# Transformer block with expert retrieval on one core: the last sublayer and the query run once per 128-token tile, the second tile on plain float32 weights

## The chip, the cores and the metric

The kernel runs on one core of one Trainium2 chip. The metric is the device time of one execution in microseconds (us), the median of several runs. It is written by hand: each engine has its own program, and the engines meet only at semaphores. TensorE (PE) does the matrix products, VectorE (DVE) and ScalarE (ACT) the elementwise work, GpSimd (POOL) and SyncE (SP) issue transfers.

## The reference, cut to what matters

256 tokens of width 2048 pass through two layers of a first block (layers 0 and 1 below), then a mixer sublayer and a retrieval sublayer of a second block. 16 meta tokens stand ahead of the tokens in the second block. The change touches only the second block:

```
h = x;  16 meta tokens ahead of it
proj = rms_norm(h) @ w_in            # 2048 x 7176: sb_q sb_k sb_v fq fk fv fgate flogit
sb   = stick_breaking_attention(...)  # 8 heads of 128, causal
fox  = forgetting_attention(...)      # 8 heads of 128, causal, q and k normed per head
h    = h + concat(rms_norm(sb), rms_norm(fox) * sigmoid(fgate)) @ w_out      # 2048 x 2048
hb   = rms_norm(h)
q    = hb @ w_query                   # 2048 x 2048 -> 8 heads, 2 halves of 128
s    = q . sub_keys;  top 16 of each half, top 16 of the 256 sums -> idx (8 heads x 16), g = softmax
a    = gelu(u[idx] . hb);  out = h + sum (g * a) * v[idx]                    # u, v: 16384 x 2048
```

Attention is causal, so the first 128 tokens need nothing of the last 128.

## The kernel before, in words

**Passes.** Seven products of all 256 tokens with a weight matrix follow each other, numbered p = 0 to 6: `w_in` and `w_out` of layer 0 and 1 (p 0 to 3), then `w_in_2` (4), `w_out_2` (5) and the query weights (6). `GROUPS` cuts the columns of each into groups of up to 512; `PIECES` cuts each group into 8 pieces of 256 rows. A piece is one load of 512 KB (256 rows x 512 columns) into one of the 4 slots of `ring` (SP queue). `split` on ACT copies it to `wH` (float32r, a rounded float), `split` on DVE writes the rest, raw minus `wH`, to `wL`; there are three buffers of each (`NB`). `piece` on PE then makes each product as three float32r products (`three`: high by high, high by low, low by high) for the two token tiles t = 0 and 1, into banks `pp`. The left factor, `hH` and `hL`, is made ahead by `chunk` (PE transposes, ACT rounds, DVE subtracts), four rows of 128 at a time. SP's wait is for a free ring slot: a slot is free when DVE has split it, and in the key and value groups of p 4 only when PE has also read it for the meta tokens (`piece_meta`, plain float32 on the raw weights).

**Order.** One generator, `order`, is walked by all five engine programs. Between the pieces `pump` steps the lanes X, Y and M, generators that do the attention a little at a time: `stick` and `fox_pair` in p 4, both tiles together. All engines are in order, so an engine that waits in a lane step holds up its next piece.

**Retrieval.** `scores` and `choose` find the experts for a group of 32 picks per token (i = 0 to 7; i // 4 is the tile). `dot` is a gather of 128 rows of `u` (1 MiB, an indirect transfer that POOL issues) and one DVE multiply-and-sum of 128x2048; `vmix` is four such gathers of `v` and 16 PE products. Each gather takes one of `NG` = 11 slots `gs`. There are 256 gathers of u and 256 of v. The first 20 dots stand beside the last pieces of p 6, all else after them. `hidden` makes the normed tokens `hn` that a dot needs, `blend` the weights of a vmix.

Of the kernel before, what the change touches and what calls it, by code (L numbers as in the profile page):

```python
# [27 lines left out]
GBP, FHP = (QI, 6144)  # L28
NP = 6488
SQ, SK, SV, FQ, FK, FV, FG, FL = (0, 1024, 2048, 3072, 4096, 5120, 6144, 7168)  # L30
MSK, MSV, MFK, MFV, MFL = (0, 1024, 2048, 3072, 4096)

ID, ONE, TRL, TRU, NTT, SM, NSM, INV, CUT, SEL, ROW, NCW = (0, 128, 256, 384, 512, 640, 768, 896, 976, 980, 996, 1000)
# [5 lines left out]
def constants():  # L39
# [14 lines left out]
    cw[:, SEL:SEL + 16] = (i[:, None] % 32) == 16 + np.arange(16)[None, :]  # L54
# [95 lines left out]
def cgroups(*spans):  # L150
# [23 lines left out]

def order():

    owed = {"X": 0.0, "Y": 0.0, "M": 0.0}
    where = [(p, q) for p in range(7) for q in range(len(PIECES[p]))]
# [15 lines left out]
    def project(p, after, rates, early, beside=lambda n, pc: ()):  # L194
        for q, (n, c0, w, pc) in enumerate(PIECES[p]):
# [5 lines left out]
            if p == 4 and meta_part(c0, w):  # L201
                yield "meta", p, q
# [9 lines left out]
            if p == 4 and n == 0 and pc == 1:  # L212
                yield "chunk", p, 3
            yield from pump(*rates(n))

    LATE = {1: {2: 3}, 3: {2: 3}, 5: {1: 2, 3: 3}}
# [64 lines left out]
    def after_in2(n):  # L281
        if n == 2:
            yield "open", "X", "forget"
        if n in (3, 9):
            yield "open", "Y", "stick", n // 9
        if n in (4, 10):
            yield "open", "X", "fox_turn", n // 10, FQ
        if n in (6, 12):
            yield "open", "X", "fox", n // 12
        if n == 13:  # L290
            yield "open", "X", "fox_rms"
        if n == 14:
            yield "drain", "X", "Y"
            yield "fox_gate",

    def beside_in2(n, pc):
        if n == 0 and pc == 3:
            yield "norm", 4
        if n and pc == 3:
            yield "drain", "M"  # L300
        if n in (6, 12) and pc == 3:
            yield "open", "X", "fox_turn", n // 12, FK

    def early_out2(pc):
        if pc == 1:
            yield "drain", "Y"
            yield "chunk", 5, 0
        if pc == 3:
            yield "chunk", 5, 1
# [14 lines left out]
    for q, (g, c0, w, pc) in enumerate(PIECES[6]):  # L324
        yield from splits(6, q)
        if q == 3:
            yield "norm", 6
# [2153 lines left out]
```

## Time and profile before

| | |
|---|---|
| runs | 3119.54, 3122.51, 3128.95 us (median 3122.51) |
| profiled execution, first to last instruction | 3121.8 us |
| PE, DVE, ACT, POOL busy | 67%, 59%, 27%, 26% of the span |
| moved by the transfers | 900.90 MB |
| p 4 begins on PE | 1157.5 us |
| first gather | 1797.4 us |
| last gather lands | 3110.8 us |

The span of 3121.8 us is 0.7 us under the median of the runs, so sums made on the profiled execution stand for the runs as well. "Beside" means on another engine or queue in the same stretch. A MATMUL row's duration is longer than the distance to the next one, since products overlap in the array; a stream is priced by the distance of starts. A plain float32 product shows as two rows, a float32r product as one.

### The profile page before, as it was taken

Reading aid. Unit: us, or ns where it says so; the run is one execution under the profiler, and the core shown is the slowest. Engines: PE = TensorE matmul, PEld = TensorE weight load, DVE = VectorE, ACT = ScalarE, POOL = GpSimd, SP = SyncE. Lnnn points to the kernel's source line nnn. Section 1 sums busy time; section 2 is a strip of 40 time slices with the busy share of each in tenths; the row PEclk is TensorE's granted clock in tenths of the full one; section 3 lists DMA queues with packets and bytes.
Section 4 is the critical chain, followed back from the end, with each engine's and each line's share of the span. In section 5 each row is a group of like instructions: output and inputs, shape, how many; then the busy total and the mean of one; then the engine's idle time right before and its main releaser. Section 6 shows DMA issues by size and latency. Waiting matters only on the chain.

```text
span 3121.8 us, 29077 instructions
## 1 busy us (share of the span) xinstructions
PE 2089.0 (67%) x11378; PEld 1478.6 (47%) x11378; DVE 1836.5 (59%) x2711; ACT 853.8 (27%) x1267; POOL 800.9 (26%) x680
## 2 busy tenths in 40 slices
PE   5888989989999999999999983223232322322235
PEld 2676777888787787666668871000000000000001
DVE  3679886566776664343336697766565555564430
ACT  1334544444454454544545420000000000000000
POOL 1111110000000000000000036665555555555552
PEclk8999999999999999999999996566656566666667
DMA  9887875557665545334226699999999999999998
GB/s 385 289 293 263 296 259 150 184 182 248 210 189 153 164 158 172 111 122 132 85 82 201 194 377 403 422 422 421 421 422 421 422 421 419 421 421 421 421 421 346
DMA packets 244741, 900.90 MB, mean 289 GB/s; under 512 B 20759, under 2 KB 45613, under 8 KB 178413
## 3 DMA queue, kind: packets, MB, share of 16 engines
q0 software_dynamic: 94208, 612.85, 48.9%
q1 hardware_dynamic: 149152, 284.53, 27.8%
q8 instruction: 90, 1.47, 0.2%
q10 hardware_dynamic: 1244, 1.67, 0.2%
q14 instruction: 47, 0.38, 0.0%
HBM read 894.78 MB, written 2.10 MB: 287 GB/s over the span
## 4 chain that ended last, share of the span: by engine, by line
PE 45%; DMA 29%; DVE 10%; ACT 3%; issue 3%; POOL 2%; ACTq 0%; POOLq 0%; DVEq 0%
PE pp L1818 38%; DMA late<-in_peer_v,MI 9%; DMA P<-in_peer_v,MI 5%; PE tp L1818 5%; DMA x<-in_peer_v,MI 5%; DMA ring<-in_peer_v,MI 4%; DVE wL L1130 3%; DMA SY<-in_peer_v,MI 2%; PE tp L1821 2%; ACT wH L626 1%; DMA ring<-in_peer_w_query 1%; DVE UHM L1286 1%; DMA ring<-in_w_in 1%; POOL late L2361 1%; DVE P L1777 0%
## 5 line engine op out<-in xcount | busy, mean ns | idle before, releaser
L1130 DVE TENSOR_TENSOR wL<-ring,wH 128x1024 fp32r<-128x1024 f32 (+3 forms) x504 | 583.2, 1161 | 573.7 <-ACT wH L626 572.4
L1818 PE MATMUL pp<-wH,hH 128*128 128x512 f32 (+3 forms) x1888 | 745.7, 395 | 35.5 <-DVE wL L1130 19.4
L1818 PE MATMUL pp<-wL,hH 128*128 128x512 f32 (+3 forms) x1888 | 721.4, 382 | 0.0
L1818 PE MATMUL pp<-wH,hL 128*128 128x512 f32 (+3 forms) x1888 | 720.5, 382 | 0.0
L626 ACT ACTIVATE wH<-ring 128x1024 fp32r<-128x1024 f32 (+3 forms) x504 | 508.3, 1011 | 729.7 <-PE pp L1818 548.0
L1818 PE MATMUL pp<-late,S 128*32 128x512 f32 x768 | 232.6, 879 | 335.7 <-DMA x<-in_peer_v,MI 156.3
L1818 PEld LDWEIGHTS pp<-wH,hH 128*128 128x128 f32 x1888 | 362.3, 192 | 141.2 <-issue 46.3
L1818 PEld LDWEIGHTS pp<-wH,hL 128*128 128x128 f32 x1888 | 361.6, 192 | 64.1
L1818 PEld LDWEIGHTS pp<-wL,hH 128*128 128x128 f32 x1888 | 362.8, 192 | 57.3 <-issue 1.0
L1777 DVE CUSTOM_DVE_ANT_0 late<-late,P 128x2048 f32<-128x2048 f32 x84 | 191.2, 2288 | 155.2 <-DMA late<-in_peer_u,MI 155.2
L1818 PE MATMUL pp<-P,S 128*32 128x512 f32 x360 | 162.7, 898 | 166.9 <-DMA late<-in_peer_v,MI 93.2
L1818 PEld LDWEIGHTS pp<-late,S 128*32 128x32 f32 x768 | 52.1, 154 | 441.3 <-issue 441.3
L1818 PE MATMUL pp<-ring,S 128*32 128x512 f32 x344 | 156.7, 890 | 142.3 <-DMA late<-in_peer_v,MI 142.3
L1818 PE MATMUL pp<-x,S 128*32 128x512 f32 x376 | 165.1, 880 | 126.2 <-DMA P<-in_peer_v,MI 65.8
L2371 POOL DMA_DIRECT2D P<-in_w_mod x85 | 44.9, 529 | 634.2 <-DVE hL L1173 314.3
L1818 PE MATMUL pp<-SY,S 128*32 128x512 f32 x200 | 140.3, 867 | 89.8 <-DMA P<-in_peer_v,MI 89.8
L1029 ACT ACTIVATE MI<-MI 128x32 f32<-128x32 f32 x8 | 1.8, 229 | 640.3 <-DVE MI L1697 640.3
L1777 DVE CUSTOM_DVE_ANT_0 P<-P 128x2048 f32<-128x2048 f32 x53 | 121.0, 2288 | 93.4 <-DMA P<-in_peer_u,MI 93.2
L2361 POOL DMA_INDIRECT late<-in_peer_v,MI x96 | 117.6, 1225 | 173.5 <-PE pp L1818 149.4
L1777 DVE CUSTOM_DVE_ANT_0 x<-x,P 128x2048 f32<-128x2048 f32 x49 | 111.9, 2289 | 78.9 <-DMA x<-in_peer_u,MI 78.9
L2347 POOL DMA_DIRECT2D UHM<-in_norm_ffn x1 | 0.5, 533 | 605.6 <-PE pp L1818 605.6
L1777 DVE CUSTOM_DVE_ANT_0 ring<-ring,P 128x2048 f32<-128x2048 f32 x47 | 107.2, 2288 | 75.7 <-DMA ring<-in_peer_u,MI 75.7
(305 smaller groups left out, 2985.2 us busy)
## 6 DMA issues: line engine op xcount, KB each, us to landing
ring<-in_w_in SPq DMA_DIRECT2D x288, 512.0 KB, 4.4
ring<-in_w_out SPq DMA_DIRECT2D x96, 512.0 KB, 4.2
P<-in_w_mod POOLq DMA_DIRECT2D x85, 512.0 KB, 5.1
late<-in_w_mod SPq DMA_DIRECT2D x64, 512.0 KB, 9.4
SY<-in_w_mod POOLq DMA_DIRECT2D x43, 512.0 KB, 5.5
ring<-in_w_in SPq DMA_DIRECT2D x48, 368.0 KB, 4.8
ring<-in_peer_w_query SPq DMA_DIRECT2D x32, 512.0 KB, 7.9
ring<-in_w_in SPq DMA_DIRECT2D x24, 344.0 KB, 3.2
```

The costliest lines, as they stand in the source:

```text
L626: act(heads(wH[k % NB][:, 0:2 * wd], 2), raw, ACT.Copy).then_inc(*tick("act_hi", ("hi", k)))
L1029: act(c3, c3, ACT.Exp).then_inc(*tick("act_x", ("gap exp", i)))
L1130: tt(lo, raw, hi.bitcast(F32), ALU.subtract).then_inc(*tick("dve_lo", *names))
L1286: stt(mod_acc, wv, c, mod_acc, ALU.mult, ALU.add).then_inc(*tick("dve_side", *names))
L1777: e.tensor_tensor_reduce(out=gs[slot], in0=gs[slot], in1=hn[i // 4], scale=1.0, scalar=0.0, op0=ALU.mult, op1=ALU.add, accum_out=aa[i % 2] ...
L1818: return e.matmul(o, l, r, start=start, stop=stop, skip_group_check=skip)
L1821: return e.transpose(o, i, ident[0:k, 0:k])
L2347: e.dma_start(to, src).then_inc(*landed(sem, *names))
L2361: e.indirect_dma_start(gs[slot], None, tab[0], bass.IndirectOffsetOnAxis(ap=picks, axis=0)).then_inc(*landed(f"expert_in{slot}", ("gathere ...
L2371: e.dma_start(mod_in[b], I["w_mod"][l, k * 128:(k + 1) * 128, c0:c0 + 1024]).then_inc(*landed(f"mod_in{b}", ("mod", m)))
```

## The change

Passes 4 to 6 become six passes of one tile each: 4, 5, 6 for tokens 0 to 127, then 7, 8, 9 for tokens 128 to 255, over the same three weight matrices, which are so loaded twice. Groups are 1024 columns wide (the first 344, one 688), and a piece is one row block of 128 by the group's width: 16 pieces to a group, 192 pieces a tile. Tile 0 keeps the split into `wH` and `wL`. Tile 1 has no split: its pieces multiply the raw weights in `ring` by `hB`, float32. The attention lanes do four heads (tile 0) or two (tile 1) of one tile at a time in both lanes. In passes 7 to 9, 128 dots (all u gathers of tile 0) are dealt out at 0.68 to a piece; for them there are 6 gather slots, and 13 after pass 9. Scores, choice, `hidden` and the transposed sub-keys are made per tile; the v gathers of tile 0 come after pass 9.

```diff
-G_IN2 = cgroups((FG + 688, 1, 344), *[(c + 512 * h, 1, 512) for h in range(2) for c in (SQ, SK, SV, FQ, FK, FV)],
-                (FG, 2, 344))
-GROUPS = [G_IN, G_OUT, G_IN, G_OUT, G_IN2, G_OUT, G_OUT]
-PIECES = [[(n, c0, w, pc) for n, (c0, w) in enumerate(g) for pc in range(8)] for g in GROUPS]
-NB, NS, NG = 3, 4, 11
-FIRST_DOT = 12
+G_IN2 = [(FG + 688, 344), (FQ, 1024), (FK, 1024), (FV, 1024), (FG, 688), (SQ, 1024), (SK, 1024), (SV, 1024)]
+G_OUT2 = [(0, 1024), (1024, 1024)]
+GROUPS = [G_IN, G_OUT, G_IN, G_OUT, G_IN2, G_OUT2, G_OUT2, G_IN2, G_OUT2, G_OUT2]
+BOTH = 4
+NPC = [8] * BOTH + [16] * 6
+NB, NS, NG = 3, 4, 13
+SHARE = 0.68
...
+    def dot(share):
+        dots[1] += share
+        while dots[1] >= 1:
+            dots[1] -= 1
+            if dots[0] < 32 * min(chosen[0], 4):
+                yield "dot", dots[0] // 32, dots[0] % 32
...
+    for p in (4, 7):
+        t, share = tile_of(p), 0 if p == 4 else SHARE
+        for q, (n, c0, w, pc) in enumerate(PIECES[p]):
...
+            if p == 7 and (n, pc) == (0, 8):
+                yield from choice(1)
+            yield "piece", p, q
...
+            yield from pump(*((0.8, 0.8, 1) if p == 4 else (0.7, 0.7, 1)))
+            yield from dot(share)
...
+            if n == 0 and pc == 3:
+                for k in range(14 if t else 0):
+                    yield "step", "X"
+                    yield "step", "Y"
+                    yield from dot(1)
+                yield "drain", "X", "Y"
+                yield "open", "Y", "stick_norm", t
...
+    yield "rest",
+    yield "turn_q", 9, 1
+    yield "scores", 6
+    yield "scores", 7
+    yield "open", "X", "choose", 4
+    yield "blend", 0
+    for b in range(8):
+        yield "vmix", 0, b
...
+        hB = late[:, 2048:4096].rearrange("p (k n) -> p k n", k=NK)
...
             def split(p, q):
                 n, c0, wd, pc = PIECES[p][q]
-                r, k = next(loads), next(cut)
-                raw = heads(ring[:, r % NS, 0:2 * wd], 2)
+                r = next(loads)
+                if p >= 7:
+                    return
+                k, size = next(cut), 2 * wd if p < BOTH else wd
...
+            def piece_one(p, q):
+                n, c0, wd, pc = PIECES[p][q]
+                k, r, kk = next(cut) if p < 7 else None, raw_of[p, q], row_of(p, n, pc)
+                w.wait_ge(*(at("lo", k) if p < 7 else at("raw", r)))
+                w.wait_ge(*at("chunk", p, kk // 4))
+                for j, (o, wj) in enumerate(sides(wd)):
+                    b = bank_of(p, n, j)
+                    if pc == 0 and b in had_bank:
+                        w.wait_ge(*at(*had_bank[b]))
+                    if p < 7:
+                        m = three(pp[b][:, 0:wj], (hA[0][:, kk, :], hA[1][:, kk, :]),
+                                  (wH[k % NB][:, o:o + wj], wL[k % NB][:, o:o + wj]), pc == 0, pc == 15)
+                    else:
+                        m = mm(pp[b][:, 0:wj], hB[:, kk, :], ring[:, r % NS, o:o + wj], pc == 0, pc == 15)
...
                 if before is not None:
                     w.wait_ge(*at("expert used", before))
-                elif slot in (3, 4):
+                elif slot < 6:
+                    w.wait_ge(*at("grouped", 6, 1, 1))
...
+                else:
+                    w.wait_ge(*at("grouped", 9, 1, 1))
```

## Rows read from the trace of the kernel before

**Rows 1.** The page: engines in 40 equal slices of the span.

```profile
PE   5888989989999999999999983223232322322235
DVE  3679886566776664343336697766565555564430
PEclk8999999999999999999999996566656566666667
GB/s 385 289 293 263 296 259 150 184 182 248 210 189 153 164 158 172 111 122 132 85 82 201 194 377 403 422 422 421 421 422 421 422 421 419 421 421 421 421 421 346
```

**Rows 2.** Busy time by stretch: PE, weight loads, DVE, ACT, POOL; clock, transfer share, GB/s.

```profile
1157.50:1180.00 22.50, 21.77 (x154) 19.29 (x154) 14.26 (x32) 12.35 (x23) 0.00 (x0) 1.00 0.58 186
1180.00:1655.00 475.00, 451.73 (x2186) 326.51 (x2185) 178.84 (x272) 229.85 (x362) 0.00 (x0) 0.96 0.36 113
1655.00:1740.00 85.00, 84.68 (x408) 71.59 (x407) 51.92 (x61) 41.61 (x59) 1.06 (x2) 1.00 0.69 222
1740.00:1797.40 57.40, 54.06 (x383) 50.88 (x381) 41.70 (x90) 25.14 (x35) 4.10 (x9) 0.97 0.60 184
1797.40:1866.00 68.60, 55.51 (x396) 53.20 (x397) 62.07 (x86) 18.71 (x19) 24.79 (x19) 0.90 0.99 385
1866.00:3110.80 1244.80, 381.11 (x2158) 110.16 (x2157) 688.34 (x1005) 27.85 (x38) 689.19 (x493) 0.64 1.01 418
```

**Rows 3.** Timeline of PE at 1077 us: one float32r stream of 512 columns.

```profile
1076.87 0.39 PE L1818 MATMUL pp<-wH,hL 128*128 128x512 f32 x1
1077.10 0.39 PE L1818 MATMUL pp<-wH,hH 128*128 128x512 f32 x1
1077.32 0.39 PE L1818 MATMUL pp<-wL,hH 128*128 128x512 f32 x1
```

**Rows 4.** Timeline of PE at 511 us: two plain float32 products of 512 columns.

```profile
511.00 1.99 PE L1818 MATMUL tp<-S,CW 128*128 128x512 f32 x4 [0.95 <-DVE S L1105]
513.06 0.39 PE L1818 MATMUL pp<-wL,hH 128*128 128x512 f32 x1
```

**Rows 5.** Groups of 1180 to 1655 us: splits, meta products, attention's small products.

```profile
L1130 DVE TENSOR_TENSOR wL<-ring,wH 128x1024 fp32r<-128x1024 f32 x94 | 115.2, 1226 | 236.9 <-ACT wH L626 236.7
L626 ACT ACTIVATE wH<-ring 128x1024 fp32r<-128x1024 f32 x93 | 98.5, 1060 | 163.3 <-PE pp L1818 98.4 <-DMA ring<-in_w_in 64.5
L1818 PE MATMUL pp<-ring,UHM 128*32 128x512 f32 x256 | 40.0, 618 | 0.0
L1818 PE MATMUL tp<-P,SY 128*128 128x128 f32 x60 | 13.1, 333 | 4.0 <-ACT SY L917 4.0
L1821 PE MATMUL tp<-CW,P 128*128 128x128 f32 x80 | 11.2, 286 | 6.9 <-issue 2.9 <-ACT P L772 2.5 <-ACT P L704 1.6
```

**Rows 6.** Timeline of ACT at 1694 us: the split's distance when PE paces it.

```profile
1693.84 1.06 ACT L626 ACTIVATE wH<-ring 128x1024 fp32r<-128x1024 f32 x1 [1.66 <-PE pp L1818]
1696.56 1.06 ACT L626 ACTIVATE wH<-ring 128x1024 fp32r<-128x1024 f32 x1 [1.66 <-PE pp L1818]
```

**Rows 7.** Transfers by tile: loads of the ring, and their time to landing.

```profile
L564 SPq DMA_DIRECT2D ring<-in_w_out x96: 367/368/813, 540.7 to 1736.6; - x96
...
DMA to landing us min/median/max: 3.4/4.2/7.9
```

**Rows 8.** Busy time by stretch as in rows 2: 20 to 80 and 560 to 640 us.

```profile
20.00:80.00 60.00, 43.35 (x659) 18.92 (x648) 25.39 (x50) 12.08 (x26) 0.00 (x0) 0.83 1.03 408
560.00:640.00 80.00, 80.00 (x356) 65.51 (x355) 44.86 (x47) 36.01 (x45) 0.00 (x0) 1.00 0.56 182
```

**Rows 9.** Timeline of DVE at 1820 us: the dot beside the split.

```profile
1818.66 2.29 DVE L1777 CUSTOM_DVE_ANT_0 SY<-SY,P 128x2048 f32<-128x2048 f32 x1
1820.87 1.22 DVE L1130 TENSOR_TENSOR wL<-ring,wH 128x1024 fp32r<-128x1024 f32 x1
1822.01 2.29 DVE L1777 CUSTOM_DVE_ANT_0 x<-x,P 128x2048 f32<-128x2048 f32 x1
```

**Rows 10.** Timeline of DVE: first and last row of the first choice.

```profile
1784.80 0.29 DVE L1636 MAX8 MI<-UHM 128x8 f32<-128x128 f32 x1 [1.26 <-ACT UHM L1084]
1810.30 0.19 DVE L1705 TENSOR_TENSOR MI<-MI 128x32 f32<-128x32 f32 x1
```

**Rows 11.** The chain that ended last, late pieces: start, us, what.

```profile
2998.37 13.15 DMA P<-in_peer_v,MI
3011.65 5.07 PE pp L1818 x32
3026.89 14.44 DMA P<-in_peer_v,MI
```

**Rows 12.** Timeline of PE in the gathers' stretch: the pace of products after a pause.

```profile
2014.63 1.07 PE L1818 MATMUL pp<-late,S 128*32 128x512 f32 x2 [19.75 <-DMA x<-in_peer_v,MI]
2015.46 1.10 PE L1818 MATMUL pp<-late,S 128*32 128x512 f32 x2
2017.84 0.61 PE L1818 MATMUL pp<-late,S 128*32 128x512 f32 x2
2018.27 0.61 PE L1818 MATMUL pp<-late,S 128*32 128x512 f32 x2
```

More of the change, by code:

```diff
@@ L344, in order, with choice @@
-    for i in range(8):
+    dots, chosen = [0, 0.0], [0]
+    def dot(share):
[4 more added lines that the diff above has]
+                yield "dot", dots[0] // 32, dots[0] % 32
+                if dots[0] >= 32 and dots[0] % 32 == 3:
+                    yield "gelu", dots[0] // 32 - 1
+                dots[0] += 1
+    def choice(i):
+        if i:
+            yield "drain", "M"
+        chosen[0] = i
+        if i < 4:
+            yield "open", "M", "choose", i
@@ L345, in order @@
+    yield "rest",
[6 more added lines that the diff above has]
+        yield "vmix", 0, b
+        yield from dot(4)
+        yield from pump(1.5, 0, 0)
+    while dots[0] < 128:
+        yield from dot(1)
+        yield from pump(1, 0, 0)
+    yield "gelu", 3
+    yield "drain", "X"
+    for i in range(4, 8):
         if i < 7:
-            yield "scores", i + 1
             yield "open", "X", "choose", i + 1
-        for j in range(0 if i else 32 - FIRST_DOT, 32):
+        for j in range(32):
@@ new lines, in turn_four @@
+                u = next(turn)
+                w.wait_ge(*at("turned", u))
+                if t == 0:
+                    act(mkt[:, 0 if names == "stick" else 1, 4 * half:4 * half + 4, :], heads(tp[u % 2][:, 512:576], 4), ACT.Copy,
+                        scale=kk).then_inc(*tick(R.act))
+                act(R.H[:, 512:1024 + 512 * t], tp[u % 2][:, 0:512 + 512 * t], ACT.Copy, scale=kk).then_inc(
+                    *tick(R.act, ("pair free", u), (names + " keys", *meta)))
+                yield
@@ new lines, in stick_a, with stick_v @@
+                act(z, z, ACT.Exp).then_inc(*tick(R.act))
+                w.wait_ge(*at("stick log", t, half, g, 1))
+                act(zm, zm, ACT.Exp).then_inc(*tick(R.act, ("stick weights", t, half, g)))
+                yield
+            def stick_v(lane, half, t, g):
+                R, hg = ROOM[lane], 4 >> t
+                yield
+                u = next(turn)
+                w.wait_ge(*at("turned", u))
+                o = YS + (4 * half + hg * g) * 128
+                act(P[:, t, o:o + hg * 128], tp[u % 2][:, 0:hg * 128], ACT.Copy).then_inc(
+                    *tick(R.act, ("pair free", u), ("mixed heads", t, half, g)))
+                yield
@@ new lines, in fox @@
+                    w.wait_ge(*at("fox weights", t, half, g))
+                    w.wait_ge(*at("stored", p, 3, 1))
+                    if t == 0:
+                        w.wait_ge(*at("meta out", 3))
+                    for h in range(hg):
+                        c, o = (4 * half + hg * g + h) * 128, pr[:, h * 128:(h + 1) * 128]
+                        mm(o, pm[:, h * 128:(h + 1) * 128], PM[:, MFV + c:MFV + c + 128], True, False)
+                        for kt in range(t + 1):
+                            i = h * (t + 1) + kt
+                            m = mm(o, pT[:, i * 128:(i + 1) * 128], P[:, kt, VF + c:VF + c + 128], False, kt == t)
```

1332 lines of the change are left out of this document (671 added, 661 removed).

## The prediction

> **What bounds the kernel now.** I read the page's slices first [rows 1]. PE is at nine tenths up to slice 23, then falls to two or three tenths, while the transfers rise from under 210 GB/s to 422 and stay there. So the kernel has two limits in turn: PE's work first, then the rate of the gathers. The stretches [rows 2] say how much: from 1180 to 1655 us PE is busy 451.7 of 475 us and the transfers 0.36; from 1866 to 3110.8 us the transfers move 418 GB/s at a share of 1.01, PE is busy 381 of 1245 us. The chain [rows 11] shows the second stretch as a landing of v, 5 to 6 us of PE, the next landing. What the gathers have to wait for is the first expert choice at 1797.4 us; all transfer capacity ahead of it that the weights don't use is lost. The change takes gathers into that stretch, and pays by loading 92 MB again. Thus the new time is a sum of stages: the start (unchanged), tile 0's pass, tile 1's pass with 128 gathers beside it, the rest.
>
> **Start.** Passes 0 to 3 keep their code; p 4 starts at 1157.5 us [rows 2].
>
> **Tile 0's pass, PE's work.** A float32r product of 512 columns takes 0.228 us from start to start [rows 3]. The three matrices have 7176 + 2048 + 2048 = 11272 columns in 16 row blocks; three products each give 11272/512 x 16 x 3 x 0.228 = 241 us for one tile, half of before. The products for the meta tokens stay: 256 rows, four at a time in the array. Their 40 us busy [rows 5] overlap others; by distance, 64 sets at the 0.427 us of a plain pass, 27 us, and I take 30 with the narrow ones. In 1180 to 1655 us the main products are 96 x 2.73 + 16 x 1.84 = 291 us (a 512-wide and a 344-wide piece), so of PE's 451.7 us some 133 are attention and its transposes for both tiles. They are small: 0.14 to 0.22 us busy for each row of 128 columns [rows 5]. By the count of such products in the new lanes (160 of about 0.2 us and 5 us of long ones for tile 0, 216 and 10 us for tile 1) tile 0 has 37 us and tile 1 55; transposes, queries and sub-keys add 18 us to each, and tile 0's meta selection and forget sums some 10. Tile 0: 241 + 30 + 37 + 18 + 10 = 336 us.
>
> **Tile 0's pass, its stalls.** A piece now takes PE 6 x 0.228 = 1.37 us, not 2.73, but the split of its 128x1024 words costs ACT 1.06 and DVE 1.23 us as before [rows 5]. With three buffers a split can start when the piece three before it is done, and must be through when two more are: 1.06 + 1.23 + 0.2 of handing over = 2.5 us against 2.73 of PE. Before, ACT started every 2.72 us and sat idle 1.66 of it [rows 6]; that slack is gone, and each attention operation on ACT or DVE now delays a split. The ring adds a second loop: landing 3.4 us at least and 4.2 in the median [rows 7], and the split, make 6 to 6.7 us for a slot, with four slots 1.5 to 1.7 us a piece, and about 2 us in the 64 key and value pieces whose slots wait for the meta products. Before, PE was busy 97% of 1157.5 to 1797.4 us (612 of 640, rows 2). I take 87%: 336 / 0.87 = 385 us. The bounds: 345 (still 97%), and 450, if all 160 wide pieces take 2.5 us (PE's 1.37, the lanes' 0.4, and a split no longer hidden) and the 32 narrow ones 1.5. The work hidden is DVE's 192 splits (216 us) and 60 us of lanes, ACT's 187 + 75: under 75% of 385.
>
> **Tile 1's pass.** Its load is 92.4 MB of weights and 128 gathers of 1.049 MB, 134.2 MB. The weights' rows in memory are 4 KB now (2 KB before); loads with such rows (w_mod at 20 to 80 us) ran at 408 GB/s [rows 8], and the gathers at 418 [rows 2]. 92.4/0.408 + 134.2/0.418 = 226 + 321 = 547 us. At the other end, 385 GB/s, the mixed stretch at 1797 to 1866 us [rows 2], gives 589. PE's work: a plain float32 product shows as two rows [rows 4]; four rows, two products, take 1.7 us ahead of the next stream, 0.855 us each at 2.4 GHz. That is 11272/512 x 16 x 0.855 = 301 us, more than the 241 of the split way, and with 55 + 18 + 12 (choice's scores, forget sums) 386 us. DVE loses the splits and gets 128 dots at 2.29 us [rows 9], 293 us, three choices of about 22 us (25.7 us first to last row [rows 10], three splits of 1.2 taken off), 66, and lanes and sums of 45: 404 us. So neither engine sets the pass while the clock holds, and the transfers do. The attention's drains can starve them: at pass 8 the lanes take 14 steps each with no pieces between, but six gather slots and four ring slots are 8 MB, 20 us of transfers, and dots go on there. I add 18 us: 565.
>
> At which clock? Between 20 and 80 us PE was 72% busy in short bursts and the granted clock 0.83 [rows 8]; at 1797 to 1866 us, 81% and 0.90 [rows 2]. At 0.83 a 386 us sum becomes some 450, still under 565. After the 20 us pauses in the gathers' stretch the distances fall from 0.85 to 0.43 us [rows 12], the levels 1.2 and 2.4 GHz. The Trainium skill, "TensorE: Matmul & The Clock Gate", section "HAM oscillation — how this bites in real kernels", speaks against the change: a loop over k-tiles of few rows that waits for a transfer at each k-tile runs them at half clock every time. Here each of the 16 row blocks is such a wait. By that rule PE's sum would double; it is the third rival below.
>
> **Handover and rest.** At 0.68 a piece from the ninth piece on, and 14 extra, the 128th dot falls on the sixteenth piece of pass 9, and its gather up to six slots earlier. Some 20 pieces follow with weights alone, at PE's 1.71 to 1.9 us for 0.52 MB, where the transfers could do it in 1.28; and no gather can start until pass 9 gives slot 6 back (it holds `hB`), then one must land. I take 20 us, bounds 10 and 40. Then 384 gathers: 402.7 MB / 0.418 = 963 us, and 11 us from the last landing to the end, as before. What the moved waits hold up: POOL's queue stands at the first gather until pass 6 is done, with nothing behind it but gathers; SP's queue has 192 more loads behind the ring's slots; DVE, waiting for a gather in a dot, holds up the attention steps behind it and through them PE.
>
> **Sum.** 1157.5 + 385 + 565 + 20 + 963 + 11 = 3101.5 us of span, 3102 with the 0.7 us to the runs' median. The change wins some 20 us of 3122: it brings 255 us of idle transfer time to use (640 - 385), and pays 226 for the second load and about 10 more in waits.
>
> **The rivals.**
> 1. *The split chain sets tile 0's pass.* The price of its loops is the one I know least. At 430 us, 2.2 us a piece, the sum is 3147. The point from which the change is slower is 405 us, PE at 83%. For it: slack falls from 1.66 us to 0.2; the ring's loop for key and value pieces is as long as PE's work there. Against: ACT and DVE are each under 75% used. This ends on the other side.
> 2. *PE-bound and clean, gathers full.* Tile 0 at 350, tile 1 at 550, handover 12: 3044 us. For it: 97% in rows 2. Against: the slack above.
> 3. *Half clock in tile 1's pass.* 301 + 85 doubled is 772 us: 3309. For it: the clock of 0.64 in rows 2 where PE waits for transfers. Against: waits are then 14 us long, here about 1 us, and rows 8 grant 0.83 at 72%. A clock of 0.7 gives 551 us and changes nothing; it decides below about 0.68.
> 4. *The gathers are not kept up in tile 1's pass*, because DVE in order waits for a dot while the lanes wait for DVE: at an effective 350 GB/s it takes 647 us, and the end is 3184.
>
> **How the numbers follow.** My forecast (3065 to 3140) has 0.58, rival 1 beyond it 0.14, rival 2 0.15, rival 3 0.05, rival 4 0.08. About 0.3% (9 us) is what a measurement of this kernel can tell from no change. Faster, under 3113: rival 2 and about two thirds of the forecast's own chance, 0.55. Within: 0.14. Slower, over 3131: rivals 1, 3, 4 and a little of the forecast's upper end, 0.31. The range 3045 to 3175 leaves out rival 3, half of 4 and the ends.
>
> **What would show it.** After: the first u gather at about 1545 us; tile 0's stretch with PE busy 85 to 90% and DVE waiting for ACT less than before; transfers of 995 MB in all; tile 1's stretch with over 395 GB/s, PE rows of 0.43 us distance and a clock over 0.8; pass 9 done near 2120 us; then 418 GB/s to the end with 384 gathers. Wrong if the first gather comes after 1565 us (step "stalls"), if tile 1's stretch shows under 380 GB/s while ring and gather slots are idle, or a clock under 0.7.

## The result, and the profile after

The change makes the kernel slower: 3238.69 us median of four runs (3230.73 to 3240.88) beside 3121.03 us for the kernel before on the same chip, a ratio of 1.0376 with a 95% interval of 1.0351 to 1.04. The forecast was 3102 us, faster, with a range of 3045 to 3175. The profiled execution took 3239.1 us, 117.3 more than the 3121.8 of before. These are its slices, to be laid beside those of before [rows 1]:

```profile
PE   6888989989999988888767767458522322223555
DVE  3678886567865555445789655636065556544000
POOL 1111100000000000000013333521455555555332
PEclk8999999999999989998989999789766666666777
GB/s 386 282 292 265 307 225 155 182 224 205 232 160 147 179 178 203 188 167 201 255 324 411 395 389 372 360 304 306 418 421 422 421 422 422 421 422 422 421 421 369
```

The gathers now begin in slice 20 and the transfers stand near 400 GB/s from slice 21 on, as meant. But from slice 14 on, counted from 0, PE shows no nine, and slices 25 to 27 (2024 to 2267 us) fall to 360, 304 and 306 GB/s, with PE at four, five and eight tenths beside them. The stretches answer to [rows 2] (PE, weight loads, DVE, ACT, POOL; clock, share of transfers, GB/s):

```profile
1157.50:1633.00 475.50, 395.68 (x1729) 260.13 (x1728) 276.33 (x409) 261.64 (x383) 1.06 (x2) 0.92 0.61 200
1633.00:1700.00 67.00, 43.70 (x112) 20.02 (x112) 55.60 (x153) 4.02 (x8) 15.48 (x16) 0.82 0.96 370
1700.00:1800.00 100.00, 66.69 (x150) 25.00 (x150) 91.49 (x179) 13.20 (x30) 38.99 (x26) 0.98 1.02 412
1800.00:1900.00 100.00, 78.16 (x270) 42.44 (x271) 57.34 (x68) 19.59 (x45) 37.28 (x24) 0.97 0.99 400
1900.00:2012.00 112.00, 81.63 (x218) 33.93 (x217) 57.77 (x68) 22.61 (x41) 29.44 (x21) 0.97 0.96 377
2012.00:2111.00 99.00, 56.63 (x167) 26.25 (x165) 65.23 (x78) 20.27 (x43) 58.48 (x27) 0.81 0.89 355
2111.00:2187.00 76.00, 39.30 (x88) 16.89 (x88) 27.85 (x26) 3.56 (x12) 19.13 (x11) 0.80 0.78 297
2187.00:2232.00 45.00, 31.93 (x71) 12.49 (x71) 31.06 (x40) 3.73 (x12) 13.69 (x13) 0.96 0.97 372
2232.00:2265.50 33.50, 31.87 (x91) 14.80 (x89) 17.88 (x67) 4.43 (x7) 0.00 (x0) 1.00 0.69 229
2265.50:3239.00 973.50, 368.77 (x2072) 96.88 (x2072) 359.88 (x498) 15.08 (x21) 479.55 (x384) 0.67 1.00 416
```

Two rows cut the span into the stages of the prediction. The first row of u, in POOL's timeline:

```profile
1633.00 1.02 POOL L2479 DMA_INDIRECT late<-in_peer_u,UHM  x1 [128.68 <-DVE MI L1742]
```

The first row of v, by tile (count: ns min/median/max, first and last start):

```profile
L2479 POOL DMA_INDIRECT late<-in_peer_v,UHM x134: 934/940/2371, 2265.5 to 3194.8; - x134
```

The start is 1157.5 us as before. Tile 0's pass takes 1633.0 - 1157.5 = 475.5 us (385 in the sum), tile 1's pass with the handover 2265.5 - 1633.0 = 632.5 (585 in the sum), the rest 973.6 (974 in the sum). So 90 and 47 us are off, in two stages, and nothing elsewhere. The 995 MB are as forecast. Two of the prediction's own signs of being wrong came: the first gather after 1565 us, and rates under 380 GB/s in tile 1's pass.

What ends ACT's and PE's idle time in tile 0's pass, in the view of waits (us in total, times, longest):

```profile
ACT wH L721 <- DMA ring<-in_w_in: 97.3, 67, 4.9
ACT wH L721 <- PE pp L1909: 36.6, 40, 4.3
ACT wH L721 <- DMA ring<-in_w_out: 22.4, 11, 10.6
PE pp L1909 <- DVE wL L1231: 55.1, 49, 5.8
```

PE waits for a split, and the split for a load. Before, ACT's splits waited more for PE than for loads (98.4 and 64.5 us in [rows 5]). In tile 1's pass PE's longest waits are:

```profile
PE pp L1909 <- DMA ring<-in_w_in: 103.4, 67, 3.5
PE tp L1912 <- DVE P L1203: 25.8, 1, 25.8
PE pp L1909 <- DMA ring<-in_w_out: 24.0, 13, 4.2
PE tp L1912 <- DMA ring<-in_peer_sub_keys: 23.9, 2, 15.0
```

The two single long ones lie in pass 8, where the timeline of PE has them:

```profile
2077.11 1.08 PE L1912 MATMUL tp<-CW,P 128*128 128x128 f32 x4 [25.75 <-DVE P L1203]
2131.10 1.97 PE L1912 MATMUL tp<-CW,ring 128*128 128x128 f32 x8 [8.86 <-DMA ring<-in_peer_sub_keys]
2156.18 1.94 PE L1912 MATMUL tp<-CW,ring 128*128 128x128 f32 x8 [14.99 <-DMA ring<-in_peer_sub_keys]
```

The first waits behind the dots that stand between the stick steps. The sub-keys' load is issued only at the step that uses it, behind three loads of pieces.

### The profile page after: what moved, and what is told of

It reads as the page before. It is cut to its first block, busy times and chain, and to the rows that moved or that the text cites. A ratio compares the mean times of both kernels' runs of the same rounds, so it can differ in the third digit from the quotient of the medians.

```text
span 3239.1 us, 27902 instructions
## 1 busy us (share of the span) xinstructions
PE 2228.4 (69%) x10616; PEld 1392.6 (43%) x10616; DVE 1834.6 (57%) x2746; ACT 863.8 (27%) x1333; POOL 775.1 (24%) x681
## 4 chain that ended last, share of the span: by engine, by line
PE 33%; DMA 31%; DVE 12%; POOL 6%; issue 6%; ACT 3%; POOLq 0%; ACTq 0%; DVEq 0%
PE pp L1909 27%; DMA ring<-in_w_in 8%; DMA late<-in_peer_v,UHM 8%; PE tp L1909 5%; DMA ring<-in_peer_v,UHM 4%; DMA x<-in_peer_v,UHM 4%; DVE wL L1231 4%; POOL late L2479 3%; DMA P<-in_peer_v,UHM 3%; DMA ring<-in_w_out 2%; ACT wH L721 2%; PE tp L1912 1%; DVE late L1869 1%; POOL P L2479 1%; DVE UHM L1403 1%
## 5 line engine op out<-in xcount | busy, mean ns | idle before, releaser
L1231 DVE TENSOR_TENSOR wL<-ring,wH 128x1024 fp32r<-128x1024 f32 (+4 forms) x512 | 582.0, 1145 | 428.4 <-ACT wH L721 425.3
L1909 PE MATMUL pp<-wH,hH 128*128 128x512 f32 (+3 forms) x1648 | 666.7, 405 | 89.1 <-DVE wL L1231 68.8
L721 ACT ACTIVATE wH<-ring 128x1024 fp32r<-128x1024 f32 (+4 forms) x512 | 507.3, 995 | 622.9 <-PE pp L1909 439.6
L1909 PE MATMUL pp<-wL,hH 128*128 128x512 f32 (+3 forms) x1648 | 636.5, 386 | 0.0
L1909 PE MATMUL pp<-wH,hL 128*128 128x512 f32 (+3 forms) x1648 | 636.2, 386 | 0.0
L2479 POOL DMA_INDIRECT late<-in_peer_u,UHM x198 | 315.5, 1593 | 621.6 <-DVE UHM L1869 322.1
L1909 PE MATMUL pp<-ring,late 128*128 128x512 f32 (+1 forms) x736 | 354.0, 618 | 142.6 <-DMA ring<-in_w_in 103.4
L1909 PEld LDWEIGHTS pp<-wH,hL 128*128 128x128 f32 x1648 | 320.0, 194 | 57.8
L1869 DVE CUSTOM_DVE_ANT_0 late<-late,UHM 128x2048 f32<-128x2048 f32 x128 | 288.5, 2284 | 47.2 <-DMA late<-in_peer_u,UHM 47.1
L1909 PEld LDWEIGHTS pp<-ring,late 128*128 128x128 f32 x736 | 136.4, 200 | 339.3 <-DMA ring<-in_w_in 165.7
L2479 POOL DMA_INDIRECT late<-in_peer_v,UHM x134 | 137.9, 1029 | 173.2 <-PE pp L1909 137.3
```

The source lines that it names most:

```text
L721: act(wH[k % NB][:, 0:size], ring[:, r % NS, 0:size], ACT.Copy).then_inc(*tick("act_hi", ("hi", k)))
L1231: tt(lo, raw, hi.bitcast(F32), ALU.subtract).then_inc(*tick("dve_lo", *names))
L1869: e.tensor_tensor_reduce(out=gs[slot], in0=gs[slot], in1=hn[i // 4], scale=1.0, scalar=0.0, op0=ALU.mult, op1=ALU.add, accum_out=aa[i][:, ...
L1909: return e.matmul(o, l, r, start=start, stop=stop, skip_group_check=skip)
L2479: e.indirect_dma_start(gs[slot], None, tab[0], bass.IndirectOffsetOnAxis(ap=picks, axis=0)).then_inc(*landed(f"expert_in{slot}", ("gathere ...
```

## The experiments

The times below are read at the same two marks. "Pass 0" is from 1157.5 us to the first row of u, "pass 1" from there to the first row of v. "After" is the changed kernel. Medians are of four runs each, ratios against runs of the kernel before on the same chip. The runs were made on several chips, where the kernel before took 3121.0 to 3129.4 us in the median; so a difference of a few us between two rows is read from the passes and the ratios as well.

| run | median us | ratio (95%) | profiled | pass 0 | pass 1 | rest |
|---|---|---|---|---|---|---|
| after | 3238.69 | 1.0376 (1.0351 to 1.04) | 3239.1 | 475.5 | 632.5 | 973.6 |
| e1_ring8 | 3181.55 | 1.0173 (1.0143 to 1.0204) | 3184.8 | 417.7 | 634.7 | 974.9 |
| e2_plain0 | 3216.14 | 1.0286 (1.0255 to 1.0317) | 3215.3 | 451.1 | 633.1 | 973.6 |
| e3_noattn | 3156.53 | 1.0095 (1.0059 to 1.0131) | 3156.2 | 409.0 | 615.5 | 974.2 |
| e4_nodots | 3355.04 | 1.0721 (1.0687 to 1.0756) | 3356.2 | 475.5 | 429 | 1294 |
| e5_draindots | 3235.6 | 1.0337 (1.0319 to 1.0355) | 3238.8 | 476.2 | 629.9 | 975.2 |
| e6_subearly | 3224.07 | 1.0301 (1.0284 to 1.0319) | 3224.3 | 472.8 | 619.4 | 974.6 |
| e7_both | 3217.54 | 1.0288 (1.0271 to 1.0305) | 3211.2 | 467.8 | 611.7 | 974.2 |
| e8_ring8_both | 3161.82 | 1.011 (1.0094 to 1.0127) | 3155.6 | 410.7 | 613.7 | 973.7 |
| e9_ring8_plain0 | 3190.44 | 1.0213 (1.0178 to 1.0248) | 3188.1 | 423.5 | 632.6 | 974.5 |
| e10_v_early | 3155.96 | 1.0104 (1.0082 to 1.0126) | 3152.7 | 411.7 | 568.9 | 1014.6 |
| e11_half_drain | 3161.23 | 1.0125 (1.0104 to 1.0147) | 3155.5 | 410.5 | 567.5 | 1020.0 |
| e12_ring8_noattn | 3102.11 | 0.9933 (0.991 to 0.9957) | 3100.5 | 355.2 | 613.6 | 974.2 |
| e13_nb4 | 3266.21 | 1.0455 (1.0429 to 1.0482) | 3259.0 | 496.2 | 630.3 | 975.0 |
| e14_best_nb5 | 3157.63 | 1.0101 (1.0083 to 1.012) | 3151.7 | 412.6 | 567.0 | 1014.6 |
| e15_share35 | 3227.33 | 1.0338 (1.0302 to 1.0375) | 3224.5 | 414.6 | 519.8 | 1132.6 |
| e16_share52 | 3195.1 | 1.0225 (1.0199 to 1.0251) | 3187.8 | 406.6 | 567.5 | 1056.2 |
| e17_half_ring6 | 3187.07 | 1.0208 (1.0185 to 1.0231) | 3183.7 | 412.3 | 481.4 | 1132.5 |
| e18_all_ring6 | 3146.17 | 1.0069 (1.0052 to 1.0085) | 3145.4 | 416.9 | 597.2 | 973.8 |

In e4 the second mark is where tile 1's pass ends (2062 us), since no row of u is fetched in it, and its first mark is taken from "after". In e10, e11 and e14 rows of v are fetched ahead of pass 9's end, in e15 to e17 dots of u follow the pass, so their last two columns count together.

### Tile 0's pass: the ring, the splits, the attention

Four more slots for the ring in passes 4 to 6, in the half of `P` that is tile 1's:

```diff
+            i = RING[r][0]
+            return ring[:, i, :] if i < 4 else P[:, 1, 1024 * (i - 4):1024 * (i - 3)]
```

> The changed kernel with eight ring slots in place of four in passes 4 to 6 (the other four lie in P[:, 1, 0:4096], which tile 0's pass does not use). In the changed kernel tile 0's pass takes 475.5 us (1157.5 to 1633), and ScalarE waits 97 us in 67 waits for ring loads of w_in there, about 22 us for w_out and 16 us for query rows. Theory ring (a slot comes free only when its piece is split, so the next load lands too late): most of that is on the path, the pass falls to 400 to 430 us, the meta groups from 70 us to about 55, and the total to 3165 to 3195. Rival lanes and split chain (ScalarE would wait for VectorE or TensorE instead): the pass stays at 460 to 475 us, the total at 3225 to 3240, and the time of those waits turns up under other releasers.

The ring's theory holds, in the pass and in the total (3182): 57.8 us less in pass 0. No load is left among what ACT's splits wait for longest; the releaser is PE, as it mostly was before the change. The waits, and the stretch:

```profile
ACT wH L747 <- PE pp L1935: 104.6, 135, 7.7
PE pp L1935 <- DVE wL L1257: 27.2, 22, 2.9
```

```profile
1157.50:1575.00 417.50, 377.96 (x1728) 258.44 (x1726) 275.17 (x407) 261.77 (x383) 1.06 (x2) 0.94 0.66 226
```

PE is 91% busy instead of 83%. Its busy time itself falls by 18 us, at a clock of 0.94 for 0.92.

Tile 0 on plain float32, TensorE reading the ring:

```diff
-                    if p < 7:
-                        m = three(pp[b][:, 0:wj], (hA[0][:, kk, :], hA[1][:, kk, :]),
...
+                    m = mm(pp[b][:, 0:wj], (hC if p < 7 else hB)[:, kk, :], ring[:, r % NS, o:o + wj], pc == 0, pc == 15)
```

> The changed kernel with tile 0's pass on plain float32 weights and stationary chunks too: its 1024-wide and 512-wide pieces are no longer split (about 230 splits on ScalarE and as many on VectorE gone), and TensorE reads the ring slot. The main products of tile 0 cost about 288 of 0.855 us = 246 us for 0.228 x 3 x 288 = 197 us, and the meta products stay. Theory split chain (VectorE's 1.15 us and ScalarE's split, with the attention steps between them, set the time of a piece): tile 0's pass falls below 440 us, the total to about 3200. Rival TensorE (its own products, waits of its own chains included, set it): the pass rises by about 50 to 520 us and the total to about 3290. Rival ring (loads set it): the pass stays near 475 us, as a slot is now held until the product is done.

Between the theories: pass 0 falls by 24 us, so it is neither the ring alone (it would have stayed) nor the products (it would have risen). TensorE is busy 426.7 of 450.5 us. PE idles 24 us in place of 80. With no splits in the loop, the dearer products cost less than the waits did. With both edits:

> Eight ring slots in passes 4 to 6, and tile 0's pass on plain float32 weights as well, with no splits. Tile 0's pass took 417.7 us with eight slots, 451 with plain float32 and four slots, where TensorE was 427 us busy. Theory TensorE (with a ring deep enough the splits are hidden, and the pass is TensorE's own work): the plain products cost what the split saved, tile 0's pass is 430 to 445 us, and the total 3195 to 3215, slower than with eight slots alone. Rival split chain (the splits still cost 20 us or more with eight slots): the pass is 400 to 415 us, the total under 3182.

```profile
1157.50:1581.00 423.50, 420.13 (x1366) 189.09 (x1364) 61.92 (x199) 82.64 (x194) 1.06 (x2) 0.96 0.67 222
```

TensorE is busy 99%. The pass is pure TensorE work, 6 us longer than with the splits, where PE works 42 us less and idles 36 us more. It came out 6 us under the range of the TensorE theory, and slower than with eight slots alone, as that theory had it. The splits save work and give nearly all of it back in waits: of PE's 80 us of idle time in "after", the four further slots take 40, and leaving out the splits takes 36 more.

More split buffers, first with four ring slots (`wH`, `wL` in the unused halves of `hH`, `hL`, four pieces ahead), then with eight and five pieces ahead:

```diff
+            for bufs, b in ((wH, hH), (wL, hL)):
+                bufs.append(b[:, :, :].rearrange("p k n -> p (k n)")[:, spare:spare + 1024])
```

> The changed kernel with four ring slots as it is, and one split issued further ahead in passes 4 and 5: five pairs of buffers wH, wL in place of three (the other two lie in the halves of hH and hL that one tile's stationary leaves free), four pieces ahead. Theory ring (slots, not split buffers, set tile 0's pass with four slots): it stays within 10 us of 475 us, the total at 3225 to 3240. Rival split chain (three buffers are too few when a piece takes TensorE 1.37 us): the pass falls by 25 us or more, the total under 3215.

> e10_v_early (eight ring slots, no dots in pass 8's drain, sub-keys early, first v gathers early: 3156 us) with five pairs of split buffers and five pieces ahead in passes 4 and 5. There tile 0's pass takes 411 us, TensorE is 91% busy, and with plain float32 weights and eight slots it was 99% busy. Theory split chain (what is left of TensorE's idle time comes from splits that stand behind the attention's steps on ScalarE and VectorE): half to all of 38 us goes, total 3120 to 3140. Rival order (the splits are issued in a fixed order with the attention's steps, so that more buffers don't bring them earlier): less than 8 us, total over 3148.

The first is 21 us slower in pass 0, which neither theory had: ACT's splits stand one place further ahead in its order, and it waits for their loads, 165 us in all, with steps that PE needs behind it. The second changes nothing (412.6 for 411.7). So it is not the number of split buffers that was short. The splits do cost idle time (e9 shows 36 us of it); that they cost it by the fixed order of ACT's and DVE's steps is argued, not shown.

The attention left out, with four and with eight slots:

> The changed kernel without the heads' attention in both tiles: the transposes of queries and keys, the logits, the exponentials, the sums and the weighted values of both lanes are left out on all three engines, what follows reads what lies in those places, and the rest stands. TensorE's work in it was put at 37 us for tile 0. If the attention costs its TensorE time alone, tile 0's pass falls by 35 to 45 us to 430 to 440. Theory stalls (its short steps on ScalarE and VectorE stand between the splits of the weights, which delays the pieces behind them): the pass falls by 70 to 110 us, near the 385 us predicted. Rival: it is hidden behind loads and splits, and the pass stays at 460 or more. In tile 1's pass the stick steps at the head of pass 8 go too, where TensorE waits 26 us for VectorE: there 25 to 60 us should go.

> Eight ring slots in passes 4 to 6, and the heads' attention of both tiles left out as in e3_noattn (its logits, exponentials, sums and weighted values; what follows reads what lies in those places). With four slots leaving it out cut tile 0's pass from 475 to 409 us, TensorE's busy time by 53. Theory TensorE (with eight slots the pass is TensorE's work at 90%): 418 less 53 to 60 is 358 to 365 us. Rival two bounds (without attention the ring or the split chain sets the pass, whose weights alone need 226 us of transfers): over 375 us. Total 3115 to 3125 by the first (with the 17 us that tile 1 lost in e3_noattn), 3130 to 3145 by the second.

Pass 0 falls by 66.5 and 62.5 us, of which PE's busy time is 53.5 (395.7 to 342.2) with four slots and 57.6 (378.0 to 320.3) with eight. With four slots that lies between the expectations (a fall of 35 to 45, or of 70 to 110); with eight the TensorE theory's 358 to 365 us was missed by 3, and its total by 13. In tile 1's pass 17 to 21 us go, less than the 25 to 60 expected. So leaving out tile 0's attention takes 63 to 67 us, 54 to 58 of them PE's busy time, not 37. The ring's gain with the attention out is 53.8 us (409.0 to 355.2), with it 57.8: the two gains nearly add. The 9% of idle time with eight slots stays near 10% without attention (320.3 of 355.2).

### Tile 1's pass: what a gather beside it costs

> The changed kernel with none of tile 0's dot products beside tile 1's pass: all 128 of them, and with them the gathers beyond the ring's depth, follow the pass. Nothing else is moved. Theory transfers (tile 1's pass of 632 us is set by 92 MB of weights and 134 MB of gathers): with the weights alone the pass is TensorE's, 400 to 460 us, and the whole loses what the overlap had won: 134 MB at 418 GB/s is 321 us more behind it, the total is 3360 to 3400. Rival (TensorE and the vector work set tile 1's pass, and gathers only fill its gaps): the pass stays above 550 us and the total is 3450 or more.

```profile
1633.00:2062.00 429.00, 391.25 (x1168) 191.67 (x1168) 102.56 (x357) 87.01 (x192) 4.97 (x10) 0.97 0.68 224
2062.00:3356.00 1294.00, 374.31 (x2072) 97.83 (x2072) 666.78 (x824) 16.69 (x24) 745.01 (x512) 0.62 1.00 417
```

The pass is inside the theory's range, the total (3355) 5 us below it. Tile 1's pass alone takes 429 us with PE busy 391; the sum had put PE's work at 386. From here the account of the change can be closed. Before, both tiles in one pass took 639.9 us up to the first row of u, with the last pieces of p 6 still beside the gathers up to 1866 us; one tile behind the other, without gathers, takes 475.5 + 429 = 904.5, which is 264.6 more. Behind that mark 30.4 us are gained (1324.4 before, 1294 here), as no pieces are left there. So the second pass costs 234.2 us net. The overlap wins 1723 - 1606.1 = 116.9 of the 321 us that tile 0's rows of u take. 264.6 - 30.4 - 116.9 = 117.3 us, the whole of the difference.

The two waits of pass 8, alone and together, and on the deeper ring:

```diff
-                    yield from dot(1)
...
+            if (n, pc) in ((0, 15), (1, 3)):
+                yield "sub_load", t, 8 * n
```

> The changed kernel without the 14 dot products that its order puts between the stick steps at the head of pass 8; the share of dots per piece goes from 0.68 to 0.70 to make up for them. In the changed kernel TensorE waits 25.8 us there for VectorE, which works through these dots (2044 to 2073 us) before it reaches the sum that TensorE's next step needs. Theory vector order (the path goes through VectorE there): tile 1's pass falls from 632 us by 15 to 30 us, the total to 3210 to 3225. Rival transfers (the pass is set by its 226 MB): the wait goes but the time comes back as slower pieces behind it, and the total stays at 3232 to 3242.

> The changed kernel with the two loads of sub-keys of each tile issued three pieces before their use, in the place that the order of the pieces gives them in the ring, and not at the step that uses them. In the changed kernel TensorE waits 23.9 us for them in tile 1 (8.9 and 15.0) and 4.5 us in tile 0, and the queue of gathers runs empty twice meanwhile. Theory late issue (the wait is on the path, and gathers lost in it don't come back): tile 1's pass falls by 18 to 28 us, the total to 3210 to 3225. Rival transfers: the loads only move their waits to other pieces, the total stays at 3232 to 3242.

> The last two edits together: no dots between the stick steps of pass 8, and the sub-keys loaded three pieces ahead. If both waits are on the path and apart from each other, the gains add up: 40 to 55 us less, total 3185 to 3200. If transfers set tile 1's pass (92 MB of weights and 134 MB of gathers at about 410 GB/s make 552 us) the two give less together than alone, and the total is no lower than 3205.

> The same two edits on the kernel with eight ring slots in passes 4 to 6 (3182 us alone, tile 0's pass 418 us in place of 475). Tile 0's pass and tile 1's pass stand one behind the other, so the gains should add up: 3182 less 40 to 55 us is 3127 to 3142, about 0 to 0.6% above the kernel before. If the two edits give less than 20 us it stays above 3160.

The dots' wait of 25.8 us was hardly a cost: the profile is 0.3 us away, the median 3 us, as the rival had it. Without the dots PE does not wait there, but its waits for the three kinds of weight loads grow from 64.0 to 79.7 us (1900 to 2220 us). No gather slot is given back in that time either; in e8 the transfers fall to 234 GB/s from 1950 to 2000 us. The sub-keys' waits were a cost: their early load cuts them from 28.4 to 5.3 us and gives 15 us, three of them in tile 0 (in pass 1 13 us, under the 18 to 28 expected). Together the two edits give 21 us (medians), less than half of what the waits add up to, and 20 on the deeper ring, where 3127 to 3142 had been expected. Putting half of the dots back gained nothing either:

> As e10_v_early, with seven of the 14 dots back between the stick steps at the head of pass 8, one for two steps, and the share of dots per piece at 0.69. With all 14 there TensorE waited 26 us for VectorE; with none the transfers fall to 234 GB/s from 1950 to 2000 us, as no slot is given back. Theory balance (both cost, so half costs least): 4 to 8 us less than e10_v_early. Rival: the same within 3 us.

It came out 5 us above e10 in the medians, 3 in the profiles. The handover:

```diff
-                    queue = list(range(6, NG)) + queue
+                    queue = [7, 8] + queue + [6, 9, 10, 11, 12]
```

> Eight ring slots, no dots in pass 8's drain, sub-keys early (3162 us), and one more edit: the first v gathers go into the slots P[:, 0, 4096:], P[:, 1, 4096:] and the six that tile 0's dots give back, and only then into the five that pass 9 still holds. In the changed kernel GpSimd waits at the first v gather until pass 9 is done, and from 2240 to 2265 us the transfers run at 197 to 238 GB/s. Theory handover (transfers lie idle there though rows of v could already come): up to eight gathers, 8.4 MB or 20 us of transfers, go ahead of it, 10 to 18 us less, total 3142 to 3152. Rival (these gathers delay the last loads of the query weights, so that pass 9 ends later by as much): 3155 to 3165.

Eight rows of v, 20 us of transfers, now go ahead of pass 9's end, at 393 GB/s from 2100 to 2199.5 us. But POOL's next gather waits for PE until 2199.0 us, 17 us later than in e8 (2182): the query weights share the engines with them. The net gain is 3 to 6 us; the rival's total holds.

How much of the gathers to put beside the pass (0.70 in e8 is all):

> e8_ring8_both (3162 us) with half of the dots beside tile 1's pass: 0.35 a piece in place of 0.70, the other half after the pass. Tile 1's pass took 428 us with none, 614 us with all 128 gathers. Theory transfers (the pass costs its bytes at about 400 GB/s once they exceed TensorE's time): 92 MB and half of 134 MB need 390 to 400 us, under TensorE's 428, so the pass takes 440 to 460 us and the other half 160 us behind it: 600 to 620 us together, total 3148 to 3168, the same as with all. Rival contention (each gather beside the pass costs more than its own transfer, as its dots and landings delay the rest): half is better than all by over 15 us.

> As e15_share35 with 0.52 a piece, three quarters of the dots beside the pass. Theory transfers: 92 + 100 MB are 470 us of transfers and bind the pass at about 490 to 510, with 85 us of gathers behind: total 3150 to 3170. Rival contention: between e15_share35 and e8_ring8_both, with the share in even steps.

With half, neither theory: it is 66 us slower than with all. With three quarters (3195), the rival's even steps. From the first row of u to the end it takes 1723 us with none of tile 0's 128 dots beside the pass, 1652 with half, 1624 with three quarters, 1587 with all (e4, e15, e16, e8). e4 is the changed kernel without the other edits: its shallow ring in pass 0 does not touch this stage, but its sub-keys still come late, at a cost of some 13 us by e6. A gather of 2.5 us beside the pass thus wins 0.9 to 1.1 us and costs about 1.5 us of pass, from the first one on, even where the transfers are far from full. Here is e15 and with it what the loads look like, first in e4, then in e8 (the view by tile of `in_w_in`, 1700 to 1900 us):

```profile
1700.00:1800.00 100.00, 88.86 (x294) 48.75 (x293) 44.12 (x76) 25.43 (x62) 25.45 (x15) 0.93 0.85 324
1800.00:1900.00 100.00, 82.72 (x235) 36.64 (x233) 35.27 (x49) 24.79 (x45) 16.07 (x9) 1.00 0.82 295
```

```profile
DMA to landing us min/median/max: 2.9/4.5/5.3
```

```profile
DMA to landing us min/median/max: 3.0/11.8/14.1
```

A load of weights lands in 4.5 us with no gathers beside it and in 11.8 us with them. Four slots cover four pieces of PE, about 7 us at 1.71 each. With 11.8 us a ring of four gives a piece every 3 us at best, 178 GB/s, whatever the transfers could do. That is an estimate from the two medians.

The landing time grows with what is queued, whoever queued it: before the change, from 20 to 80 us, loads of 512 KB that filled the transfers by themselves (408 GB/s) landed in 9.3 us with no gather beside them. The Trainium skill, "DMA: Bandwidth & Descriptors", section "Queues, rings and completion order", says that a DMA engine takes the queues it has work for in turn, packet by packet; by that rule a load shares the engines with the gathers queued beside it, and the landing times agree, as they would with any other even sharing. If landing is the cause, a deeper ring must help most where the transfers are not full:

```diff
+            if i > 7:
+                return late[:, 12288 + 1024 * (i - 8):13312 + 1024 * (i - 8)]
...
-            had, queue, n = {}, [0, 1, 2, 3, 4, 5], 0
+            had, queue, n = {}, [0, 1, 2, 3, 4], 0
```

> e15_share35 (half of the dots beside tile 1's pass, 3227 us) with six ring slots and five gather slots in that pass: the last 2048 words of late, freed when pass 6 is done, hold two more pieces of weights. In e15 TensorE is 82 to 89% busy from 1600 to 1900 us and waits 94 us in 57 waits for ring loads, while the transfers run at only 295 to 366 GB/s; a ring load lands in 4.6 us with no gathers beside it and in 12 us with all of them, where four slots cover 7 us of TensorE. Theory latency (each gather costs TensorE time because the weights behind it land later than the ring covers): with six slots most of the 94 us goes, the time from first u to first v row falls from 520 us to 460 to 480, total 3170 to 3195. Rival vector order (the dots and their waits hold up the pass): 505 us or more, total over 3215.

> e8_ring8_both (all dots beside the pass, 3162 us) with the same six ring slots and five gather slots. There the transfers run at 393 to 403 GB/s in 1600 to 1900 us. Theory transfers (with all gathers beside it the pass is bound by its bytes, and latency costs little): within 8 us of 3162. Rival latency: 15 us less or more.

It does: 40 us of 3227 with half of the dots, inside what the latency theory said of the total (pass 1 took 481 us, one over), and 16 of 3162 with all (13 by the ratios), where the latency rival had 15 or more and the transfers theory at most 8. In e17 the view by tile and PE's waits up to 2060 us read

```profile
DMA to landing us min/median/max: 2.9/7.0/20.5
```

```profile
PE pp L1944 <- DMA ring<-in_w_in: 28.4, 19, 2.1
PE pp L1944 <- DMA late<-in_w_in: 10.6, 8, 1.8
```

against 57.6 us in 37 waits for `in_w_in` in e15. All of PE's waits for the three matrices fall from 93.6 to 65.2 us, so less than a third of them goes, not most as expected; and of the 91 us that the gathers add to the pass in e15 (519.8 for 429), 38 go. What holds the other 52 is open. Both runs have six slots for weights and five for gathers, so one gather less in the queue is part of it; the two were not tried apart. With all dots the stretch from 1600 to 1900 us now runs at 403 to 417 GB/s (393 to 403 in e8), near the 418 of the gathers alone: there the bytes bind. PE still waits once for the sub-keys in e18, 15.2 us, so that wait is not gone by the early load. e18 is the fastest complete kernel of the study, 3146.17 us, and still 0.7% above the kernel before. No complete version beat it.

## Why the prediction was wrong

**Start, rest, transfers: right.** 1157.5 us, 973.6 for 974, 995 MB.

**Tile 0's pass, PE's work: the larger of the two terms that failed.** 336 us were summed. PE was busy 395.7 us, 60 more, of the 90 us that the pass is off. Two causes have a number. The attention is 54 to 58 us by leaving it out, not 37. And the clock: 0.92 over the pass (0.97 before the change, in 639.9 us). That is an estimate of 475.5 x 0.08 = 38 us lost, if PE was busy at the lower level. Behind a wait, the timeline shows products 0.43 us apart where [rows 3] has 0.228, the levels 1.2 and 2.4 GHz:

```profile
1204.10 0.63 PE L1909 MATMUL pp<-wL,hH 128*128 128x512 f32 x1
1204.52 0.63 PE L1909 MATMUL pp<-wH,hL 128*128 128x512 f32 x1
1204.95 0.63 PE L1909 MATMUL pp<-wH,hH 128*128 128x512 f32 x1
```

336 + 17 + 38 = 391, against 395.7. The agreement is in part luck: the two causes overlap, since attention left out takes its own slow products along, and with eight slots and no attention PE is still busy 320 us where the sum without attention has 299, at a clock of 0.98. The prediction priced a lower clock in tile 1's pass alone.

**Tile 0's pass, its stalls: too small.** They were put at 49 us (336 / 0.87), and the measured idle time is 475.5 - 395.7 = 80, 31 more. The loops were named, and each was shown short enough on its own: 1.5 to 1.7 us a piece for the ring, 2 in the key and value pieces. But a mean of 1.7 us against PE's 1.37 plus the lanes was already a bound, with nothing for a late load, and I treated it as slack. Eight slots give back 57.8 us, 40 of them idle time and 18 PE's busy time at a clock of 0.94 for 0.92. So the short ring is what most of the 90 us come from; 33 us stay with eight slots. The first rival, which the prediction put at 430 us and held to be the split chain, is what came, larger. Its ring half is shown by e1. Of its split half, the three buffers were not the cause (e13, e14), but the splits themselves cost 36 us of idle time with eight slots (e9). Its deciding point of 405 us holds only with the 585 us summed for tile 1's pass; with the 632.5 measured it is 358. With the attention out and eight slots, 355 us, the kernel is 0.7% faster than before, though it then lacks work that the kernel before does.

**Tile 1's pass: the engines' sums good, transfers too simple.** Without gathers PE's 386 us were 391. With them PE was busy 429.9 us at a clock of 0.91 over the pass; DVE's 404 us were 404.2. The price of 0.855 us for a plain product was right, though the rows shown in [rows 4] alone don't give it: they leave out the next stream's first row, at 512.42 us. At a clock of 0.83 the 386 us become 465, not 450; still under 565. The third rival falls: PE's waits for `in_w_in` are 1.5 us on average (103.4 us in 67) and 3.5 at most, and with them the granted clock is 0.97 to 0.98 from 1700 to 2012 us. By the Trainium skill, "TensorE: Matmul & The Clock Gate", section "HAM oscillation — how this bites in real kernels", a loop of few rows starts every k-tile at half clock when its wait for the transfer is long enough. The prediction took that for any wait; here the short waits did not do it. In pass 8, where waits of 9 to 26 us stand, the clock is 0.80, which agrees.

The terms that failed are the 547 us and the 18 of the drains, by 47 us together. The lines of stretches give where. They add up to 230.3 MB, not 226.6, since the sum left out the sub-keys, `in_norm_ffn` and the copies of `x` among others: 9 us. Up to 2012 us the transfers ran at 391 GB/s in the mean, not 414: 21 us. From 2012 to 2187 us, the stretch of pass 8, they ran at 330: 36 us lost for the 18 that were allowed. A sum of bytes over rate assumes that each queue always has a transfer ready. The ring had not: six slots are worth 16.5 us of pass 1 (e18), early sub-keys 13 (e6). The fourth rival gave 647 us at 350 GB/s, 667 with the handover; 632.5 at 364 came near that. Its mechanism, VectorE in order, is not shown: the one long wait behind the dots cost almost nothing when it was removed.

**Handover: right.** 20 us were taken for it. From 2187 to 2265.5 us 24.4 MB move, which need 59 us at 414 GB/s, so 20 are lost. Filling it with gathers gave 3 to 6 us, as POOL's next gather then came 17 us later.

**Seen together**, the forecast gave 20 us to a change that pays 234 us net for a second pass and can win at most 321. A margin of 20 in sums of that size should have been read as no forecast of the sign.

## What to carry to other kernels

Before you put transfers beside a loop that streams its operands, compare the load's landing time under that traffic (here 11.8 us, for 4.5 with the ring's loads alone) with what the ring covers (slots times the time of a piece). Bytes over bandwidth is a lower bound; here it was 47 us short, and two more slots gave back 16.5. When work per loaded piece is halved, every loop that had slack, slots first, has to be sized anew: here four more slots were worth 58 us and more split buffers nothing. A wait that the profile names is a cost only if the work behind it can then move up: of PE's waits, 25.8 us behind the dots were worth 0 to 3 us, 23 us behind the sub-keys were worth 15.

## What the runs showed of the hardware

- A ring load of `in_w_in` (512 KB for the wide pieces) landed in 4.5 us (median) with no gathers beside it (e4), in 7.0 us beside half of the gathers with six slots (e17), in 11.8 us beside all of them (e8), each from 1700 to 1900 us.
- TensorE kept a granted clock of 0.97 to 0.98 while it was 67 to 78% busy in bursts between waits of about 1.5 us (1700 to 2012 us), and fell to 0.80 where single waits of 9 to 26 us stood among them (2012 to 2187 us).
- Products of plain float32 at 128 rows with no splits kept PE 99% busy for 423.5 us at a clock of 0.96 (e9); the same pass in three float32r products with splits took 417.7 us, 91% busy, at 0.94 (e1).
